# Result written in quarters, first squares behind one transfer, sines behind the turned input, in a two-layer decoder trunk

## What is computed

```python
for layer in range(2):
    z = rms_norm(h, norm_mix[layer]) @ w_in[layer]
    u_ssm, z_conv, q, k_c, v_c, k_s, v_s, k_w, v_w, g_nsa = jnp.split(z, cuts, axis=-1)
    y = jnp.concatenate([_rms(s5_mixer(u_ssm, ...)), _rms(conv_mixer(z_conv, ...)),
                         _rms(nsa_mixer(q, k_c, v_c, ..., g_nsa, ...))], axis=-1) * mix_out_norm[layer]
    h = h + y @ w_out[layer]
    h = h + cross_attention(rms_norm(h, norm_cross[layer]), rms_norm(mem, norm_mem[layer]), ...)
    hn = rms_norm(h, norm_ffn[layer])
    h = h + (swiglu(hn, ...) if layer == 0 else moe_swiglu(hn, ...))   # top 2 of 8 experts
return h
```

## Time and profile before

| what | us |
|---|---|
| median of three runs (1403.8 to 1406.1) | 1404.94 |
| the profiled execution | 1405.65 |
| its span, from the first to the last instruction | 1403.84 |
| TensorE busy | 1304.5 |
| VectorE busy | 641.7 |
| ScalarE busy | 419.4 |
| GpSimd busy | 90.8 |

### The profile page before, as it was taken

The page is one execution under the profiler, slowest core; times in us unless marked ns, Lnnn a source line. Parts: engine busy times, 40 slices in busy tenths (PEclk is TensorE's granted clock), DMA queues, the critical chain, the costliest instruction groups (busy, mean ns, idle before and its releaser), DMA issues.

```text
span 1403.8 us, 48116 instructions
## 1 busy us (share of the span) xinstructions
PE 1304.5 (93%) x21350; PEld 1071.8 (76%) x21350; DVE 641.7 (46%) x1405; ACT 419.4 (30%) x831; POOL 90.8 (6%) x139
## 2 busy tenths in 40 slices
PE   6987897999999898879868999999999999999997
PEld 4754545777777585445548999999999999999996
DVE  6866512102422227463235555554555555455554
ACT  4424412100102112242222333333333333333332
POOL 0450000000000017100100000000000000000000
PEclk9997899899999999879978999999999999999999
DMA  8430042243341053100657999999999999999980
GB/s 358 192 121 1 2 167 112 95 180 146 124 180 60 34 234 150 61 2 0 242 227 284 428 426 426 426 427 426 426 426 426 426 426 426 426 427 426 426 367 32
DMA packets 32576, 357.66 MB, mean 255 GB/s; under 512 B 3683, under 2 KB 5347, under 8 KB 6412
## 3 DMA queue, kind: packets, MB, share of 16 engines
q1 hardware_dynamic: 30368, 353.78, 60.8%
q10 hardware_dynamic: 2156, 3.18, 0.7%
HBM read 355.88 MB, written 1.06 MB: 254 GB/s over the span
## 4 chain that ended last, share of the span: by engine, by line
PE 89%; DVE 4%; ACT 3%; issue 2%; POOL 1%; DMA 0%; DVEq 0%; ACTq 0%; POOLq 0%
PE bank L2031 28%; PE bank L1510 28%; PE bank L2047 14%; PE bank L1980 5%; PE bank L1518 2%; PE bank L2093 2%; PE bank L2018 2%; PE bank L1530 1%; PE bank L1771 1%; PE bank L1650 1%; PE bank L1833 1%; ACT ring L566 1%; PE bank L1581 0%; DVE ring L943 0%; POOL rs L845 0%
## 5 line engine op out<-in xcount | busy, mean ns | idle before, releaser
L2031 PE MATMUL bank<-R,ring 128*64 128x80 f32 x11264 | 421.7, 233 | 0.7 <-DVEq L925 0.7
L2031 PEld LDWEIGHTS bank<-R,ring 128*64 128x64 f32 x11264 | 403.1, 137 | 8.4 <-issue 8.4
L1510 PE MATMUL bank<-ring 128*128 128x256 f32 (+1 forms) x1408 | 377.1, 427 | 18.6 <-ACT ring L654 5.6
L1510 PEld LDWEIGHTS bank<-ring 128*128 128x128 f32 x1408 | 272.7, 195 | 122.5 <-issue 80.0
L816 ACT ACTIVATE ring<-ring 128x1024 f32<-128x1024 f32 x176 | 186.0, 1057 | 146.6 <-PE bank L2047 146.6
L2047 PE MATMUL bank<-zz,ring 128*64 128x80 f32 x5632 | 224.8, 233 | 0.0
L2047 PEld LDWEIGHTS bank<-zz,ring 128*64 128x64 f32 x5632 | 207.9, 137 | 0.0
L1472 DVE SCALAR_TENSOR_TENSOR zz<-zz,bank 128x80 f32<-128x80 f32 x176 | 41.9, 238 | 198.7 <-PE bank L2031 198.2
L1451 DVE COPY ring<-ring 128x1024 f32<-128x1024 f32 x177 | 121.6, 687 | 1.9 <-DVE R L1441 1.9
L1455 DVE COPY ring<-ring 128x1024 f32<-128x1024 f32 x177 | 121.5, 687 | 0.2
L812 ACT ACTIVATE X<-bank 128x80 f32<-128x80 f32 x176 | 41.8, 238 | 247.2 <-PE bank L2031 247.2
(11 more groups left out here) (295 smaller groups left out, 1016.8 us busy)
## 6 DMA issues: line engine op xcount, KB each, us to landing
ring<-moe_w_dram SPq DMA_DIRECT2D x177, 1536.0 KB, 11.1
ring<-ffn_w_dram SPq DMA_DIRECT2D x11, 3072.0 KB, 10.0
ring<-w_in_dram SPq DMA_DIRECT2D x6, 2048.0 KB, 10.2
ring<-w_out_dram SPq DMA_DIRECT2D x4, 2048.0 KB, 8.5
ring<-w_x_dram SPq DMA_DIRECT2D x2, 3072.0 KB, 10.5
ring<-w_small_dram SPq DMA_DIRECT2D x2, 2896.0 KB, 9.6
ring<-w_in_dram SPq DMA_DIRECT2D x2, 2144.0 KB, 20.3
ring<-bias_rows_dram ACTq DMA_DIRECT2D x1, 1536.0 KB, 9.1
```

What stands on the lines that cost most here:

```text
L1510: i = pe.matmul(out_ap, a, b, start=(k == 0), stop=(k == n - 1))
L2031: e = pe.matmul(pb[out_bank][c0:c0 + 64, 0:CAP], half[:, P * k + c0:P * k + c0 + 64], xg[:, k], start=(k == 0), stop=(k == KT - 1), tile_p ...
```

## The change

The change has four parts.

- **Quarters.** SyncE no longer waits for `h_final`, except inside the branch for full experts. It waits for the drained bank of each of the four pieces of the last expert's sum, in the order in which VectorE adds them, and writes each piece (128 rows of 512 numbers, 256 KB) by itself. The copy that raises `h_final` moves into VectorE's branch.
- **First squares.** `s5_bc` gets a semaphore of its own. The first exponential waits for `s5_lam` only; VectorE waits for `s5_bc` ahead of the steps that read it.
- **Sines.** The two sines move behind ScalarE's part of the turned input.
- **Three products.** TensorE gets three 128x256 products on the constants (`keep_warm`) between the wait for the constants and the wait for the tables. Their result in bank 4 is not read. The change in a few words does not name this part; the code has it.

```diff
 def plan_banks(banks):
     add = banks.add
-    add("t5", 5)
+    add("warm_first", 4, 0); add("t5", 5)
...
-            load(X[:].rearrange("p a b t -> p (a b t)")[:, 0:512], s5_bc[0], "s5_loaded")
+            load(X[:].rearrange("p a b t -> p (a b t)")[:, 0:512], s5_bc[0], "s5_bc_loaded")
...
-                act.wait_ge(sem["s5_loaded"], 16 * 2 * (l + 1))
+                act.wait_ge(sem["s5_loaded"], 16 * (l + 1))
                 act.activation(t[3], t[2], ACT.Exp).then_inc(sem["s5_act"], 1)
...
                 if l == 0:
-                    next(exps)
                     act.wait_ge(sem["par_loaded"], 16 * 2)
                 gained("mix_T", G_MIX, l, (1, 3))
+                if l == 0:
+                    next(exps)
...
-            sp.wait_ge(sem["h_final"], 1)
-            for i in range(NT):
-                sp.dma_start(out[i * P:(i + 1) * P], h[:, i]).then_inc(dma_out, 16)
-            sp.wait_ge(dma_out, 16 * NT)
+                sp.wait_ge(sem["h_final"], 1)
+            for g in (0, 2, 1, 3):
+                sp.wait_ge(banks.drain(f"sc{g}"), banks.count(f"sc{g}", E - 1, False) + 1)
+                sp.dma_start(out[g // 2 * P:g // 2 * P + P, 512 * (g % 2):512 * (g % 2) + 512],
+                             h[:, g // 2, 512 * (g % 2):512 * (g % 2) + 512]).then_inc(dma_out, 16)
+            sp.wait_ge(dma_out, 16 * 4)
...
-                dve.wait_ge(sem["s5_loaded"], 16 * 2 * (l + 1))
+                dve.wait_ge(sem["s5_loaded"], 16 * (l + 1))
...
                 br, bi = Xf[:, 0:P], Xf[:, P:2 * P]
+                dve.wait_ge(sem["s5_bc_loaded"], 16 * (l + 1))
...
             with dve.If(over > 0):
                 with dve.Fori(E, PASSES * E) as turn:
                     expert(turn)
-            dve.tensor_copy(flag[:, 1:2], flag[:, 0:1]).then_inc(sem["h_final"], 1)
+                dve.tensor_copy(flag[:, 1:2], flag[:, 0:1]).then_inc(sem["h_final"], 1)
...
+            def keep_warm(name, n):
+
+                banks.open(pe, name)
+                for _ in range(n):
+                    e = pe.matmul(ps(name)[:, 0:256], ident, cst[:, 0:256], start=True, stop=True)
+                done(name, e)
...
             pe.wait_ge(sem["par_loaded"], 16 * 2)
+            keep_warm("warm_first", 3)
             pe.wait_ge(sem["t5_loaded"], 32)
```

More of the change, by code:

```diff
@@ L417, in s5_params @@
             load(scr[:].rearrange("p a b -> p (a b)")[:, 0:408], s5_lam[l], "s5_loaded")
-            load(X[:].rearrange("p a b t -> p (a b t)")[:, 0:512], s5_bc[l], "s5_loaded")
+            load(X[:].rearrange("p a b t -> p (a b t)")[:, 0:512], s5_bc[l], "s5_bc_loaded")
         @block.sync
```

## The result

The change made the kernel slower, by little: 1408.7 us in the median of 22 runs (1403.2 to 1411.8), against 1404.93 for the kernel before in 22 runs (1403.6 to 1410.8). The ratio is 1.0021, with an interval of 1.0013 to 1.003. The forecast was 1399.6, with a range of 1397.8 to 1402.0. One execution of the kernel before (1965.9) and one of `two_queues` (1562.7) are far outside all others and are left out of the ratios and ranges.

The account below looks back on a forecast made before the run. The prediction took TensorE's work to bound most of the span, with other waits at the start and end. Gains of 4.5 us (end) and 0.85 us (start), 5.35 together, took the median 1404.94 to 1399.6; range 1397.8 to 1402.0.

Parts of the forecast that it names:

- First squares: Start, ScalarE: the exponential waits for s5_lam only, so squares start at 6.57, not 8.11, 1.54 us earlier.
- Warm-up: Start, TensorE: three products from 7.1 probably bring the turns of groups 2 and 3 to 2.4 GHz, 0.93 us saved.
- rival 1: Start: turns of groups 2 and 3 stay at 1.2 GHz, front gain 0, 4.5 us in all, 1400.4; chance 0.20.
- Sines: Start, ScalarE: table load and sines, 1.82 us, end at 17.35; VectorE's next S5 step starts 0.15 us later, at 17.4.
- the front: Start up to TensorE's first `bu` products: they start at 46.1, not 46.96, 0.85 us gained.
- rival 2: TensorE's clock falls during its wait at `bu`, costing 1.7 us; front -0.85, sum 3.65, 1401.3; chance 0.15.
- Tail: End: quarters written early; VectorE's way out of its branch ends the span at 1399.3, not 1403.84, 4.5 us gained.
- slower: TensorE's dense work behind `bu`: a lasting clock fall, 5.0 us per 10 us stretch at 1.2 GHz; chance 0.03.

Follow-up runs that it names:

- two_queues: split_tail, but ScalarE issues result quarters 2 and 3 and SyncE quarters 0 and 1; 1401.48 us, ratio 0.9967.
- change_two_wide: The change with two warm-up products of 384 columns for three of 256; 1407.24 us, ratio 1.0015.
- split_tail: The change without warm-up products and with the sines back ahead of the turned input; ran twice, 1400.88 and 1400.21 us.
- after_nowarm: The change without its three warm-up products, sines still moved; 1402.56 us, ratio 0.9981.
- layout_3_tiny: split_tail with three added products of 8 columns on TensorE, as many as the change has; 1405.68 us, ratio 1.0000.
- change_one_wide: The change with one warm-up product of 437 columns for three of 256; 1402.53 us, ratio 0.9966.
- no_branch: split_tail without the passes for experts with more than 80 tokens: flag reads, branches and bodies left out on every engine; 1400.37 us, ratio 0.9958.
- change_again: The change run a second time, same program; 1407.67 us, ratio 1.0011.

## Why the prediction was wrong

It was wrong in the sign. Against the forecast's span (1403.84 less 5.35, that is 1398.5) the profiled execution is 11.4 us longer; the median is 9.1 us above the forecast. By its own steps:

- **First squares: right.** The first square was forecast for 6.57 and came at 6.85, since `x` took 5.7 us to land for 5.3. The S5 steps of VectorE no longer held `xn`.
- **Warm-up: wrong here.** The step "the turns of groups 2 and 3 probably run at 2.4 GHz" failed. They took 2.09 for 1.04 us, though TensorE worked unbroken from 7.39, and they were as slow in the two other traces with three products. In `change_two_wide` they were fast (1.09), so an execution may or may not give this step. The clock was up for `u` in all four; but nothing waits for `u`, since the memory's turns behind it hang on another transfer. This was rival 1, with a chance of 0.20, and its price (`bu` where it was) was 0.8 too small.
- **Sines: the mechanism was right, the size off.** I had TensorE wait at `bu` behind the moved sines for 2 us; it waited 3.2. The `mag` copy came at 18.86 for 17.4, since the turned input was 0.5 us late and the turns 1.05 us slower. `bu` came at 47.77 for 46.1: besides the late `mag` copy, it started 0.26 us behind the end of the tanh, where I had 0.05. `split_tail`, with neither, has it at 45.5 (the mean of two traces), so moved sines and warm-up together cost all of the front's 1.4 us and 0.8 more. The sines alone (`after_nowarm`, 47.33) cost 1.8 of these 2.2, and fast turns (`change_two_wide`, 47.03) did not bring the forecast gain either.
- **Clock at `bu`: rival 2 happened in this trace** (2.8 us), but in only one of three with such a wait.
- **The loop's code: missed.** Neither the forecast nor a rival had it. I costed the three products by their work and by who waits for them, 0 us. Their instructions, ahead of the loop, cost 3.0 us of gap and 1.7 of clock behind it. `layout_3_tiny` shows it: 5 us for next to no work. This is the step that turned the sign: the change with one wide product, sines moved all the same, is 0.34% faster than before.
- **Tail: right in what it does, 1.0 us too large.** 4.6 us remained behind the last addition, forecast 3.6. I had VectorE's way out of its branch set the end, priced at the 2.75 us of the earlier trace rows, and a write land 2.9 us after its issue. In this trace the write was right (2.9) and something that no row names ended 1.6 us behind it. In nearly all other traces the write sets the end, 4.0 to 5.4 us behind the addition, because issue and landing are slower than I had them.
- The rest, 1.3 us, lies between 82 and 740 us, where none of the edits acts and the clock varies from run to run.

I gave 0.03 to slower, and all of it to a mechanism that did not occur. Without the gap the change would have been faster and still short of the forecast: `change_one_wide` has 1402.5 and `after_nowarm` 1402.6, outside the range too. Only with the sines back as well does the time come to 1400.5 (`split_tail`).

On the gap, the Trainium skill has a rule in "Runtime: NRT & Kernel Launch", Instruction fetch mechanics: the instructions come in blocks, one after the other, and crossing into the next costs little that shows. The gap of 2.3 to 3.0 us at the loop's head is what it would be where that is not hidden. That it depends on the number of instructions ahead is shown, and so is the instruction transfer 2.5 to 2.9 us ahead of its end. That TensorE waits for this very transfer is argued: the view does not say which engine the queue serves. Which instruction of the loop's entry starts it was not tried.

## What to carry to other kernels

Price added instructions by their place as well as by their work: in a program with hardware loops, look after every edit at the first turn of each loop for a gap that waits for nothing, on the engine whose instruction count changed. A step that was hidden under one engine's work is free only there; before moving it, follow what stands behind it up to the next place where the paths meet, here 28 us later at the `bu` products. And write results out as they are made, but price the last write by the traces of the end itself: beside the branches it was issued up to 1.6 us late and took up to 4.5 us to land, without them neither.

## What the runs showed of the hardware

- A gap at the entry of a loop on TensorE of 0, 2.89, 1.62 and 0.70 us with 1, 3, 12 and 24 tiny products added 740 us ahead of it.
- An instruction transfer 6.8 to 7.3 us ahead of that loop's first product in the ten traces without a gap, and 2.5 to 2.9 us ahead of it in the seven with one.
- A write of 256 KB landed 2.0 us after its issue where no engine left a branch (`no_branch`), and 2.5 to 4.7 where engines did; an issue took 0.33 us, or up to 2.3 (`after_nowarm`, `change_again`).
- TensorE at work from 7.4 to 7.6 us on in four traces; by the duration of its turns at the lower speed until 16 us in three of them (1.8 to 2.1 us for eight), at the higher from 11.86 in the fourth (1.09). The granted clock reads 1.00 in all of these rows.
- The mean granted clock of the same stretch of 65 us lay between 0.66 and 0.87 in different executions.
